# Two feed-forward stages of a one-core Trainium2 kernel: their first three weight slabs are multiplied one token tile at a time

## The reference

```
def swiglu(x, w_in, w_out):
    gate, up = jnp.split(x @ w_in, 2, axis=-1)
    return (jax.nn.silu(gate) * up) @ w_out

def ffn_half(s, shift, scale, gate, g_pre, g_post, w_in, w_out):
    h = swiglu(modulate(rmsnorm_2(s, g_pre), shift, scale), w_in, w_out)
    return s + 0.5 * gate * rmsnorm_2(h, g_post)
```

## Time and profile before

| what | value |
|---|---|
| median of 3 runs | 1303.24 us (1303.06 to 1305.71) |
| the profiled execution, its own time | 1301.28 us |
| its span, first to last instruction | 1299.5 us |
| mean granted TensorE clock | 0.997 of full speed |
| PE matmul busy | 1258.0 us, 97% of the span |
| PE weight load busy (PEld) | 1102.1 us, 85% |
| DVE busy | 845.4 us, 65% |
| ACT busy | 584.4 us, 45% |

### The profile page before, as it was taken

The page is one execution under the profiler, slowest core; times in us unless marked ns, Lnnn a source line. Parts: engine busy times, 40 slices in busy tenths (PEclk is TensorE's granted clock), DMA queues, the critical chain, the costliest instruction groups (busy, mean ns, idle before and its releaser), DMA issues.

```text
span 1299.5 us, 19281 instructions
## 1 busy us (share of the span) xinstructions
PE 1258.0 (97%) x7713; PEld 1102.1 (85%) x7713; DVE 845.4 (65%) x1329; ACT 584.4 (45%) x932; POOL 61.6 (5%) x73
## 2 busy tenths in 40 slices
PE   6999999999999999999999999999899999999997
PEld 6987999976888888887886998888588997999986
DVE  6886788796787777744424674367776676655544
ACT  7655545444632222222326652256334745544443
POOL 2030002000000000001000000010000000000000
PEclk9999999999999999999999999999999999999999
DMA  8444677675365578853241442333222554555562
GB/s 326 147 146 146 211 239 245 231 233 186 130 229 192 195 253 294 291 169 114 82 146 58 148 161 98 97 114 117 79 75 88 193 165 146 179 180 185 188 193 83
DMA packets 59465, 219.29 MB, mean 169 GB/s; under 512 B 6684, under 2 KB 6720, under 8 KB 58608
## 3 DMA queue, kind: packets, MB, share of 16 engines
q1 hardware_dynamic: 56736, 205.55, 47.9%
q0 software_dynamic: 2352, 11.76, 2.6%
q10 hardware_dynamic: 288, 0.75, 0.2%
HBM read 216.95 MB, written 1.07 MB: 168 GB/s over the span
## 4 chain that ended last, share of the span: by engine, by line
PE 85%; DVE 7%; ACT 5%; issue 2%; DMA 1%; POOL 0%; DVEq 0%; SPq 0%; ACTq 0%; POOLq 0%
PE ps L2034 19%; PE ps L2035 18%; PE ps L2036 18%; PE ps L2082 3%; PE ps L2084 3%; PE ps L2083 3%; PE ps L2093 3%; PE ps L2095 3%; PE ps L2094 3%; ACT hi L649 2%; DVE lo L1250 2%; PE ps L2071 1%; PE ps L2070 1%; PE ps L2072 1%; PE ps L2611 1%
## 5 line engine op out<-in xcount | busy, mean ns | idle before, releaser
L1250 DVE TENSOR_TENSOR lo<-raw,hi 128x1024 fp32r<-128x1024 f32 x315 | 387.8, 1232 | 304.6 <-ACT hi L649 304.3
L2034 PE MATMUL ps<-nh,hi 128*128 128x256 f32 (+1 forms) x1776 | 552.4, 311 | 4.6 <-DVE x L1777 2.5
L2036 PE MATMUL ps<-nl,hi 128*128 128x256 f32 (+1 forms) x1776 | 545.1, 307 | 0.0
L2035 PE MATMUL ps<-nh,lo 128*128 128x256 f32 (+1 forms) x1776 | 545.0, 307 | 0.0
L649 ACT ACTIVATE hi<-raw 128x1024 fp32r<-128x1024 f32 x315 | 332.4, 1056 | 445.1 <-PE ps L2036 250.7
L2034 PEld LDWEIGHTS ps<-nh,hi 128*128 128x128 f32 x1776 | 339.5, 191 | 34.7 <-issue 14.1
L2035 PEld LDWEIGHTS ps<-nh,lo 128*128 128x128 f32 x1776 | 339.6, 191 | 16.1 <-issue 0.7
L2036 PEld LDWEIGHTS ps<-nl,hi 128*128 128x128 f32 x1776 | 339.4, 191 | 15.2
L663 ACT ACTIVATE sg<-ps 128x256 f32<-128x256 f32 (+1 forms) x66 | 30.0, 454 | 132.6 <-PE ps L2036 132.5
L1237 DVE SCALAR_TENSOR_TENSOR raw<-raw,cvec 128x1024 f32<-128x1024 f32 x72 | 86.8, 1222 | 1.4
L2082 PE MATMUL ps<-hi,H 128*128 128x512 f32 x176 | 70.1, 398 | 4.3 <-DVE lo L1250 3.6
(11 more groups left out here) (359 smaller groups left out, 1303.9 us busy)
## 6 DMA issues: line engine op xcount, KB each, us to landing
raw<-in_up SPq DMA_DIRECT2D x132, 512.0 KB, 3.9
raw<-in_in SPq DMA_DIRECT2D x86, 512.0 KB, 3.7
raw<-in_w_ada SPq DMA_DIRECT2D x72, 512.0 KB, 4.6
raw<-in_down SPq DMA_DIRECT2D x66, 512.0 KB, 3.8
raw<-in_out SPq DMA_DIRECT2D x8, 512.0 KB, 4.0
raw<-in_hy_out SPq DMA_DIRECT2D x8, 512.0 KB, 3.8
raw<-in_da_out SPq DMA_DIRECT2D x8, 512.0 KB, 3.7
raw<-in_o SPq DMA_DIRECT2D x8, 512.0 KB, 3.8
```

What stands on the lines that cost most here:

```text
L1250: dve.tensor_tensor(lo[:, h, 0:w], raw[:, r, 0:w], hi[:, h, 0:w].bitcast(F32), ALU.subtract).then_inc(lo_done, 1)
L2034: mm(o, hi[:, h, wk], x_hi, start=first, stop=False)
L2035: mm(o, lo[:, h, wk], x_hi, start=False, stop=False)
L2036: return mm(o, hi[:, h, wk], x_lo, start=False, stop=last)
```

## The change

The first three slabs of up1 and of up3 are multiplied with tile 0 alone (128 columns a matmul), then with tile 1 alone. Tile 0's two pieces are turned ahead of them, tile 1's four between them. The orders on ACT and DVE are changed to match: tile 0's norm, pieces and remainders go ahead of tile 1's, and the splits of the slabs 1 and 2 go between them. The core of the diff:

```diff
-SQUARED = ((0, 0, 0), (0, 0, 1), (0, 1, 0), (1, 0, 0), (0, 1, 1), (1, 0, 1), (1, 1, 0), (1, 1, 1))
+SQUARED = ((0, 0, 0), (0, 0, 1), (0, 1, 0), (1, 0, 0), (1, 0, 1), (0, 1, 1), (1, 1, 0), (1, 1, 1))
...
 # ACT, up1
                 row_square("ffn1", b, SQ1 + b, row_piece(b // 2, b % 2))
                 if b % 2:
                     row_root("ffn1", b // 2, b // 2 + 1, b + 1, SQ1 + b, PART1 + b // 2, ROOT1 + b // 2)
-            pieces_rounded("ffn1", lambda: split(x.s - 1 + HL))
+                if b == 2:
+                    split(x.s - 1 + HL)
+            pieces_rounded("ffn1", (0, 1))
             split(x.s + HL)
+            pieces_rounded("ffn1", (2, 3, 4, 5))
...
 # ACT, up3
+            squared3(0, 1)
+            root3(0, 1, 2)
+            squared3(2, 3, 4)
+            root3(2, 2, 5)
+            squared3(5)
+            root3(1, 3, 6)
+            split(st["o2"][-2].s + HL)
+            pieces_rounded("pre3", (0, 1))
             split(st["o2"][-1].s + HL)
+            squared3(6, 7)
+            root3(3, 4, 8)
+            pieces_rounded("pre3", (2, 3, 4, 5))
             feed("up3")
...
 # DVE, up1
             part("ffn1", SQ1 + 2, 3, PART1 + 1)
+            split(x.s - 1 + HL)
             times_row(x, 2, xgr, row_ffn)
+            piece_remainders("ffn1", (0,))
             times_row(x, 3, xgr, row_ffn)
+            piece_remainders("ffn1", (1,))
             row_inverse("ffn1", 1, ROOT1 + 1, INV1 + 1)
             diagonal("ffn1", 2, 1, INV1 + 1)
-            piece_remainders("ffn1")
-            split(x.s - 1 + HL)
             split(x.s + HL)
+            piece_remainders("ffn1", (2, 3, 4, 5))
...
 # DVE, up3
-            part("rows2", SUM + 2, 3, PART + 1)
             gained("rows2", 2, 0, 3)
             part("rows2", SUM + 4, 4, PART + 2)
-            gained("rows2", 3, 0, 5)
-            row_inverse("rows2", 1, ROOT + 1, INV + 1)
+            part("rows2", SUM + 2, 3, PART + 1)
+            row_inverse("rows2", 1, ROOT + 2, INV + 2)
+            diagonal("rows2", 2, 0, INV + 2)
+            gained("rows2", 3, 0, 6)
+            row_inverse("rows2", 2, ROOT + 1, INV + 1)
             added_row("rows2", 2, 1, free[2])
+            split(st["o2"][-2].s + HL)
+            piece_remainders("pre3", (0,))
             added_row("rows2", 3, 1, free[3])
-            row_inverse("rows2", 2, ROOT + 2, INV + 2)
-            diagonal("rows2", 3, 0, INV + 2)
+            piece_remainders("pre3", (1,))
             part("rows2", SUM + 6, 7, PART + 3)
             next_gain(2)
+            split(st["o2"][-1].s + HL)
             next_gain(3)
             row_inverse("rows2", 3, ROOT + 3, INV + 3)
             diagonal("rows2", 4, 1, INV + 3)
-            piece_remainders("pre3")
-            for x in st["o2"][-2:]:
-                split(x.s + HL)
+            piece_remainders("pre3", (2, 3, 4, 5))
...
 # PE
+            def tile_products(x, k, tt):
+                h, wk, tk = x.s % HL, slice(k * P, k * P + P), slice(tt * P, tt * P + P)
+                mm(ps[:, x.bank, tk], hi[:, h, wk], nh[:, k, tk], start=k == 0, stop=False)
+                mm(ps[:, x.bank, tk], lo[:, h, wk], nh[:, k, tk], start=False, stop=False)
+                return mm(ps[:, x.bank, tk], hi[:, h, wk], nl[:, k, tk], start=False, stop=k == KD - 1)
...
-                for x in st_up:
+                turn(0)
+                turn(1)
+                early = st_up[:3]
+                for x in early:
                     begin(x)
                     for k in range(KD):
-                        if x.j == 0 and k % 2 == 0:
-                            pe.wait_ge(sem("nl"), since("nl", m) + 3 + k // 2)
-                        o = products(x, k, nh[:, k, x_], nl[:, k, x_], k == 0, k == KD - 1)
-                    o.then_inc(slab_used, 1)
+                        if x.j == 0 and k % 4 == 0:
+                            pe.wait_ge(sem("nl"), since("nl", m) + k // 4 + 1)
+                        tile_products(x, k, 0)
+                        if x.j == 1 and k == KD - 1:
+                            turn(2)
+                            turn(3)
+                        if x.j == 2 and k == 3:
+                            turn(4)
+                            turn(5)
+                for n, k in [(n, k) for g in range(4) for n in range(3) for k in (2 * g, 2 * g + 1)]:
+                    if n == 0 and k % 2 == 0:
+                        pe.wait_ge(sem("nl"), since("nl", m) + 3 + k // 2)
+                    o = tile_products(early[n], k, 1)
+                    if k == KD - 1:
+                        o.then_inc(slab_used, 1)
+                yield from early
+                for x in st_up[3:]:
+                    dense(x)
                     yield x
```

More of the change, by code:

```diff
@@ L704, in bank_done, with pieces_rounded @@
                     act.wait_ge(slab_used, x.s + 1)
-            def pieces_rounded(m, between):
-                for n, (bank, k0, kn, tt) in enumerate(PIECES):
+            def pieces_rounded(m, pieces):
+                for n in pieces:
+                    bank, k0, kn, tt = PIECES[n]
                     act.wait_ge(sem("piece_made"), since("piece_made", m) + n + 1)
@@ L713, in pieces_rounded @@
                        .then_inc(sem("nh"), 1)
-                    if n == 1:
-                        between()
             def square(m, k, src, scale=1.0):
@@ L1182, in _, with squared3, root3 @@
                 split(x.s + HL)
[L1183 to L1197, removed]
+            def squared3(*turns):
+                for turn in turns:
+                    kind, tt, half = SQUARED[turn]
+                    b = 2 * tt + half
+                    if kind:
+                        act.wait_ge(sem("x"), since("x", "rows2") + b + 1)
+                        row_square("rows2", turn, SUM + 4 + b, row_piece(tt, half))
+                    else:
+                        bank_done(st["o2"][-1], b, 12)
+                        row_square("rows2", turn, SUM + b, ps[:, b, :])
+            def root3(n, parts, squared):
+                row_root("rows2", n, parts, squared, SUM + 2 * n + 1, PART + n, ROOT + n)
+            squared3(0, 1)
[6 more added lines that the diff above has]
+            pieces_rounded("pre3", (0, 1))
             split(st["o2"][-1].s + HL)
+            squared3(6, 7)
+            root3(3, 4, 8)
+            pieces_rounded("pre3", (2, 3, 4, 5))
             feed("up3")
@@ L1317, in diagonal, with piece_remainders @@
                    .then_inc(sem("diag_ready"), 1)
-            def piece_remainders(m):
-                for n, (bank, k0, kn, tt) in enumerate(PIECES):
+            def piece_remainders(m, pieces):
+                for n in pieces:
+                    bank, k0, kn, tt = PIECES[n]
                     tk = slice(tt * P, tt * P + P)
@@ L1967, in added_row @@
             def added_row(m, b, n, use):
-                dve.wait_ge(sem("rinv"), since("rinv", m) + n % 4 + 1)
+                dve.wait_ge(sem("rinv"), since("rinv", m) + (1, 3)[n % 4] if m == "rows2" else since("rinv", m) + n % 4 + 1)
                 dve.wait_ge(bank_free[b], use)
@@ L2162, in turned_by, with fed @@
                 o.then_inc(sem("piece_made"), 1)
-            def fed(st_up, m):
-                for x in st_up:
+            def tile_products(x, k, tt):
[3 more added lines that the diff above has]
+                return mm(ps[:, x.bank, tk], hi[:, h, wk], nl[:, k, tk], start=False, stop=k == KD - 1)
+            def fed(st_up, m, turn):
+                turn(0)
+                turn(1)
+                early = st_up[:3]
+                for x in early:
                     begin(x)
                     for k in range(KD):
-                        if x.j == 0 and k % 2 == 0:
-                            pe.wait_ge(sem("nl"), since("nl", m) + 3 + k // 2)
-                        o = products(x, k, nh[:, k, x_], nl[:, k, x_], k == 0, k == KD - 1)
-                    o.then_inc(slab_used, 1)
+                        if x.j == 0 and k % 4 == 0:
[16 more added lines that the diff above has]
+                    dense(x)
                     yield x
@@ L2392, in _ @@
             pe.wait_ge(sem("pt_copied"), 3)
-            for n in range(len(PIECES)):
-                turned_by("ffn1", n, xgr, 0, since("xg", "ffn1"), 0, False)
-            for x in fed(st["up1"], "ffn1"):
+            for x in fed(st["up1"], "ffn1", lambda n: turned_by("ffn1", n, xgr, 0, since("xg", "ffn1"), 0, False)):
                 if x.j == 40:
@@ L2666, in _, with turn3 @@
                 shifts(n)
-            for n in range(6):
+            def turn3(n):
                 if n >= 4:
@@ L2670, in _ @@
                 turned_by("pre3", n, xgr, 2, since("xg", "rows2"), 4, True)
-            for x in fed(st["up3"], "pre3"):
+            for x in fed(st["up3"], "pre3", turn3):
                 pass
```

## The result

The changed kernel takes 1329.28 us (median of 6 runs, 1324.39 to 1330.13) against 1304.33 us before (6 runs, 1301.50 to 1305.71). The ratio is 1.019, with a 95% interval from 1.0173 to 1.0208: 25 us slower. The forecast was 1321 us, 18 us slower, in a range from 1314 to 1353. The profiled execution took 1327.59 us.

What follows compares the result with a forecast made beforehand. TensorE was taken as the bound, with no idle time in the rest of up1 and up3. Entry losses of 9.4 and 8.5 us, +17.9 together, took the profiled 1301.28 to 1319.2, median 1321 us; range 1314 to 1353.

Steps and rivals of the forecast that it cites:

- A: Both entries: narrow matmuls cost their weight load's pace, 0.111 to 0.121 us each; 1318 to 1325 us; chance 0.60.
- C: Both entries: 128-column rounded products take four times the streaming time, about 0.227 us each; 1351 us; chance 0.25.
- The price of a narrow matmul: In up1 and up3, each of 144 128-column matmuls a stage starts 0.111 us after the last, the load's pace.
- Rival B: Both entries: weight loads partly hidden, 0.060 to 0.10 us a narrow matmul; 1310 to 1314 us; chance 0.12.
- D: Both entries: narrow matmuls cost only their streaming and the earlier start wins, or within 0.2% below 0.039 us; chance 0.03.
- The entry of up1: First product at 131.9 us, second half of k at 133.25, slab 3 at 151.2 against 141.87: +9.4 us.
- The new wait ahead of slab 3: In both stages slab 0 is released late, so PE stands 1.55 us for slab 3's split.
- The entry of up3: First product at 1102.1 us instead of 1105.14, slab 3 at 1122.4 against 1113.85: +8.5 us.
- -8.5 + 238p: Both stages' loss in us, p being the step of a 128-column matmul: +17.9 with p = 0.111.
- The prize: Gaps ahead of up1 and up3: perfect overlap of the norms with matmuls is worth some 3 us, 0.2%.

Runs made afterwards that it cites:

- e3: Kernel before with only slabs 0 to 2 of up1 and up3 multiplied as two passes of 128 columns, orders and turns unchanged: 1320.33 against 1304.21 us.
- e5: Changed kernel with tile 1's pass going slab after slab, so slab 0 ends early: 1324.54 us against 1304.49 us before.
- e6: e2 with five unread 512-column matmuls put in PE's 1.23 us gap behind up3's first two turns: 1311.13 us against 1304.49 us before.
- e2: Changed kernel with up1's entry put back, so the change is at up3 alone: 1319.66 us against 1304.21 us before.
- e8: Kernel before with six unread 512-column matmuls in PE's 1.69 us gap ahead of up3's turns: 1301.32 us against 1303.58 us before.
- e4: Changed orders on ACT and DVE, but PE turns all six pieces first and multiplies 256 columns, at both entries: 1311.14 us against 1304.21 us before.
- e1: Changed kernel with up3's entry put back, so the change is at up1 alone: 1314.21 us against 1304.21 us before.
- e7: Changed kernel with only slab 0 multiplied a tile at a time, slabs 1 and 2 with 256 columns: 1313.61 us against 1304.49 us before.
- e10: Changed kernel with e5's slab-after-slab order and e6's five matmuls in up3: 1319.45 us against 1303.58 us before.
- e11: e6's five matmuls put behind the gap instead of in it, change at up3 alone: 1312.80 us against 1303.45 us before.

## Why the prediction was right, and where it was short

The direction and the main cost were right. That the range held the time is luck in part: 1329.28 lies above the 1318 to 1325 of A, the account that proved right in its steps, and the range reaches so far only because of C, which did not come true. No rival had the clock.

**The price of a narrow matmul** was right: 0.111 forecast from the loads' pace, 0.112 measured over 144 of them in e3. Rival B (partly hidden loads, 0.060 to 0.10), C (0.227) and D (below 0.039) are excluded by that row. The Trainium skill ("TensorE: Matmul & The Clock Gate", LDWEIGHTS) gave 107 ns for a load, and at the full clock that holds here within 5%. Its section on the back-to-back issue gap gave 81 ns for loads and matmuls of 128 columns in turn; that does not hold, 112 were measured in e3.

**The entry of up1** was right step by step: first product 131.87 (131.9), no stop at the second half of k (133.23, forecast 133.25), slab 3 151.33 (151.2), +9.3 to 9.5 us (+9.4).

**The new wait ahead of slab 3** was right in place and cause: 1.41 and 1.34 us (1.55 forecast), gone when slab 0 ends early (e5).

**The entry of up3** was right in its steps and wrong in its sum. First product 1102.1 was forecast against a trace whose o2 ends at 1095.97, that is 6.1 us behind it; it is 6.42. At the full clock (e6) slab 3 is 8.8 us late, 8.5 forecast. What was missing is the clock: the sum, -8.5 + 238p, takes every term at the full granted clock, as the earlier trace rows had it. In the changed kernel the stretch at half clock adds 4.9 us in the profiled execution (13.7 - 8.8), and e2 against e6 puts all that the filling saved at 15.5 - 6.6 = 9 us, with intervals of about 3 us to either side of each; e2's trace lost more there than the changed kernel's, 15.3 - 8.8 = 6.5 us ahead of slab 3, and some more behind it. For the profiled execution the account closes: 26.3 - 17.9 = 8.4 us more than forecast, of which 4.9 are this stretch and twice 1.6 the two short ones of the ledger. The one at the end of down1 need not come from the change, since kernels without the change at up1 show it in some traces (e6, e8) and not in others. The term was not mis-sized but absent; with 4.9 to 9 us for it the likeliest would have been 1326 to 1330. The mean clocks agree: 0.990 to 0.994 in the six executions after, 0.993 to 1.000 in those of before.

**The prize**, some 3 us, was never measured by itself: no run has the overlap without its price. The chance of 0.97 for slower stood on it and on the loads. That the orders by themselves are slower was not said as a sum; e4 shows it, at 7 us.

**Still open**: what exactly the clock depends on. The runs show one sequence in which it fell in all four traces that have it, and two ways of mending it. They don't show why up1, with nearly the same sequence (turns, a gap of 1.03 us, narrow matmuls), keeps the full clock in its narrow passes in the traces of the changed kernel, e1, e5, e7 and e10. Up3 has 2.75 us of unrounded shifts ahead of the turns, which up1 does not; that was not tested. And a single trace is weak evidence on the clock: some 30 us ahead of up1's entry, in a part that no run changes, eight of the fourteen traces have a stretch at half clock and six have none. The same stretch of the program in before and in e3:

```profile
98.50:105.30 6.80, 6.12 (x49) 5.18 (x50) 4.38 (x8) 2.54 (x7) 0.00 (x0) 1.00 0.49 154
98.50:105.30 6.80, 6.04 (x28) 5.82 (x30) 2.36 (x5) 0.85 (x3) 0.00 (x0) 0.50 0.43 154
```

## What to carry to other kernels

Where a wait is to be covered by cutting matmuls into halves, first read from the trace what a weight load costs with nothing to stream beside it: a matmul shorter than that costs the load. Then count the idle time that there is to win; here some 3 us, by estimate, were to be bought with 15 us of loads (e3). When an order change lets many buffers finish together at the end of a group, the next group's preparation loses its cover: finish the first one early. And new PE work behind a gap can run at half clock, as here: look at the granted clock of each new stretch, in more than one trace, before blaming a step.

## What the runs showed that I had not expected

- At the lower clock the narrow and the wide matmul cost the same. In the changed kernel a 128-column matmul starts 0.21 us after the one before (1115.53 to 1115.74) and a 256-column one too (1139.44 to 1139.65). At the full clock they are 0.112 and 0.121. A load's own record goes from 0.19 to 0.33 us (the rows below), so the load slows down with the clock too; no row here has loads alone at the lower clock.

```profile
1116.06 0.33 PEld L2187 LDWEIGHTS ps<-nl,hi 128*128 128x128 f32 x1
...
1127.85 0.19 PEld L2187 LDWEIGHTS ps<-nl,hi 128*128 128x128 f32 x1
```

- Five useless matmuls made a kernel faster: with them in the gap it lost 6.6 us against before (e6), with them behind it 9.4 (e11), without them 15.5 (e2).
- The kernel before spreads over 1300.67 to 1306.0 us in 22 executions on one chip, and the spread goes with the mean granted clock: all executions with 0.993 took 1305.5 us or more, all with 0.998 and above 1301.1 or less. So much of what looks like noise of 0.4% may be a few stretches at half clock, present in one execution and not in the next, as the eight traces of fourteen above show them; in which places the 22 differ was not traced.
